# One decoder layer on one core: cache copies, token squares, key turns and value products rearranged

## What is computed

```python
z = rms_norm(x, g_pre) @ w_in
u = z[:, :512] * sigmoid(z[:, 512:1024])          # conv group
q, keys and values of three branches, gates = the rest of z
cy = silu(layer_norm(causal_depthwise_conv(u, 31 taps)))
# attention: compressed blocks, selected blocks, window of 512, gated sum
o  = g0 * attend(q, compress(k_cmp), compress(v_cmp)) \
   + g1 * attend(q, selected blocks) + g2 * attend(q, window)
h  = x + rms_norm(concat(cy, o) @ w_out, g_post)
y  = h + rms_norm(square(relu(rms_norm(h, g_pre2) @ w_up)) @ w_down, g_post2)
```

## Time and profile before

| what | value |
|---|---|
| device time, median of 3 runs | 873.06 us (871.01 to 876.92) |
| the profiled execution's own time | 874.44 us |
| span of the profiled execution, first to last instruction | 872.3 us |
| mean granted clock of PE | 0.959 of 2.4 GHz |
| busy: PE, PEld, DVE, ACT, POOL | 795.3, 726.9, 461.5, 241.6, 324.9 us |
| DMA, mean over the span | 98 GB/s, 85.47 MB |

### The profile page before, as it was taken

One profiled execution on the slowest core, in us unless ns is written; L12 is line 12 of the kernel. 1 busy time (PEld: TensorE's weight loads), 2 busy tenths in 40 slices (PEclk: granted clock), 3 DMA queues, 4 the chain that ended last, 5 costly groups with the idle time before them and its releaser, 6 DMA issues.

```text
span 872.3 us, 15023 instructions
## 1 busy us (share of the span) xinstructions
PE 795.3 (91%) x6285; PEld 726.9 (83%) x6285; DVE 461.5 (53%) x661; ACT 241.6 (28%) x432; POOL 324.9 (37%) x119
## 2 busy tenths in 40 slices
PE   4979999998996898999896999999999999999990
PEld 3979999876675875665895999999999999999990
DVE  3839998466535465788267943472003433332217
ACT  3412422222244246777212322130000221200020
POOL 2100000111120010000172377777776777777754
PEclk9899999789997899999998999999999999999995
DMA  8443240244450089300021122222222122222102
GB/s 320 186 205 101 107 146 14 78 151 134 149 179 36 1 312 61 90 1 1 2 98 48 55 92 96 96 98 96 96 96 85 60 97 96 96 97 96 48 1 98
DMA packets 24015, 85.47 MB, mean 98 GB/s; under 512 B 7216, under 2 KB 10848, under 8 KB 16736
## 3 DMA queue, kind: packets, MB, share of 16 engines
q1 hardware_dynamic: 16736, 62.13, 22.4%
q0 software_dynamic: 3456, 16.78, 5.4%
q10 hardware_dynamic: 3776, 5.89, 1.9%
HBM read 80.51 MB, written 8.47 MB: 102 GB/s over the span
## 4 chain that ended last, share of the span: by engine, by line
PE 74%; DVE 12%; issue 5%; ACT 5%; DMA 4%; SPq 0%; DVEq 0%; ACTq 0%
PE PB L1320 26%; PE PA L1320 25%; PE PB L1595 4%; DMA wraw<-wblk_dram 3%; PE PS L1647 2%; PE PR L1448 2%; PE PR L1692 2%; DVE smx L1183 1%; PE PS L1712 1%; PE PB L1704 1%; DVE rb L812 1%; PE PS L1464 1%; DVE yC L864 1%; DMA xT<-x_fm_dram 1%; PE PA L1433 1%
## 5 line engine op out<-in xcount | busy, mean ns | idle before, releaser
L397 POOL TENSOR_TENSOR wH<-wraw,zero 128x2048 fp32r<-128x2048 f32 x33 | 118.9, 3602 | 232.2 <-PE PB L1320 205.0
L400 POOL TENSOR_TENSOR wL<-wraw,wH 128x2048 fp32r<-128x2048 f32 x33 | 159.9, 4846 | 2.6
L864 DVE SCALAR_TENSOR_TENSOR yC<-uP,vec,yC 128x512 f32<-128x512 f32 (+1 forms) x135 | 83.8, 685 | 0.1
L1253 DVE TENSOR_TENSOR hL<-h,hH 128x520 f32 (+1 forms) x32 | 52.5, 1643 | 49.2 <-ACT hH L771 49.2
L1320 PE MATMUL PA<-hL,wH 128*128 128x260 f32 x256 | 72.2, 282 | 0.0
L1320 PE MATMUL PB<-hL,wH 128*128 128x260 f32 x256 | 72.2, 282 | 0.0
L1320 PE MATMUL PA<-hH,wL 128*128 128x260 f32 x256 | 72.2, 282 | 0.0
L1320 PE MATMUL PA<-hH,wH 128*128 128x260 f32 x256 | 72.2, 282 | 0.0
L1320 PE MATMUL PB<-hH,wL 128*128 128x260 f32 x256 | 72.2, 282 | 0.0
L1320 PE MATMUL PB<-hH,wH 128*128 128x260 f32 x256 | 72.2, 282 | 0.0
L436 POOL DMA_INDIRECT rks<-pool_ks_dram,idx x8 | 8.7, 1082 | 162.6 <-PE PA L1413 117.1
(11 more groups left out here) (384 smaller groups left out, 2168.0 us busy)
## 6 DMA issues: line engine op xcount, KB each, us to landing
wraw<-wblk_dram SPq DMA_DIRECT2D x47, 1024.0 KB, 4.8
xT<-x_fm_dram SPq DMA_DIRECT2D x4, 520.0 KB, 6.1
xT<-x_fm_dram SPq DMA_DIRECT2D x1, 2080.0 KB, 10.2
y_fm_dram<-xT SPq DMA_DIRECT2D x8, 260.0 KB
rkw<-cwk_dram SPq DMA_DIRECT2D x8, 256.0 KB, 2.7
s_win_dram<-cwk_dram ACTq DMA_DIRECT2D x1, 2044.0 KB
s_win_dram<-cwv_dram ACTq DMA_DIRECT2D x1, 2044.0 KB
p_rows_dram<-ktok ACTq DMA_DIRECT2D x4, 256.0 KB, 2.4
```

The costliest lines, as they stand in the source:

```text
L397: pool.tensor_tensor(wH[s][:, :], wraw[s][:, :], zero[:, :].broadcast_to([P, BW]), ALU.add)\
L400: pool.tensor_tensor(wL[s][:, :], wraw[s][:, :], wH[s][:, :].bitcast(F32), ALU.subtract)\
L864: dve.scalar_tensor_tensor(out=dst, in0=src, scalar=w, in1=first, op0=ALU.mult, op1=ALU.add)\
L1253: dve.tensor_tensor(lo, h2[c % 2][:, :], hi.bitcast(F32), ALU.subtract).then_inc(s_hl, 1)
```

## The change

Six edits in one step. **Squares:** all four x loads are issued before the first weight block; ACT squares all eight tiles; DVE adds them in pairs; PE sums four pairs; the first block is split behind the root and the reciprocal. **Cache copies:** ACT issues one before each half of the MLP. **Key turns:** the first two turns of a sequence are issued together, into banks 0 and 1, the third two steps later into bank 0; the key scores of the second sequence move into the next unit. **Conv tail:** ACT copies the selected scores out of `PA` at the end of the key units, and the mean, the subtraction, the squares, the root, the reciprocal and the scaling move into units 4 to 7. **Value products:** chunk n of a sequence goes to partitions 32 x (n mod 4) onward with 32 columns of `PT` instead of 8; two more buffers come from the raw rows' space (`rawc`); the new token's products and the sum over the four strips become matmuls at the second attention pair. **Blocks 13 and 14** are split inside the attention. The diff, cut:

```diff
@@ tiles
+        vsel = [rks[0], rks[1]] + [t_[:, 0:1024] for t_ in (KTb0, KTb1, *rawc)]
+        vwin = [rkw[0], rkw[1]] + [t_[:, 1024:1536] for t_ in (KTb0, KTb1, *rawc)]
+        VBUF = (0, 1, 2, 3, 4, 5, 0, 1)
@@ SP
-            load_x(0)
-            load_x(1)
+            for i in range(4):
+                load_x(i)
             sp.dma_start(wraw[0][:, :], A_wblk[B_IN]).then_inc(s_raw[0], 16)
-            load_x(2)
-            load_x(3)
...
+            for b in range(4, 6):
+                sp.wait_ge(s_xt, 4 * (b + 3))
+                value_window(b)
+            for b in range(6, NS):
+                sp.wait_ge(s_dpv, b - 5)
+                value_window(b)
             sp.wait_ge(s_cmm, 8)
             load(1, 13)
             load(0, 14)
@@ ACT
-            for k in (0, 1, 2, 3, 4, 6):
+            for k in range(KT):
                 act.wait_ge(s_x[k // 2], 16)
-                if k == 4:
-                    block_hi(B_IN)
                 act.activation(psq[k][:, :], xT[:, k, :], ACT.Square).then_inc(s_sq0, 1)
             root(0, PB)
+            block_hi(B_IN)
...
-            for kv in range(2):
-                act.dma_start(A["s_win"][kv][:, 0:WIN - 1, :], A["win_rows"][kv][:, 1:WIN, :]).then_inc(s_out, 16)
...
                     x_evac(u + 1, 2 * e)
+                    if e == 1:
+                        gelu(u)
                     key_evac(2 * u + e, 2)
                     x_evac(u + 1, 2 * e + 1)
-                gelu(u)
...
             act.activation(Sw[:, 0:WIN], PB[0:64, 0, :], ACT.Copy).then_inc(s_dA, 1)
+            act.activation(Ss[:, 0:PAST].rearrange("p (a n) -> p a n", a=2), PA[0:64, :, :], ACT.Copy).then_inc(s_dA, 1)
...
-            for b in (13, 14):
-                block_hi(b)
...
-            act.activation(od[:, :].rearrange("p (a b) -> p a b", a=2), PS[0:8, :, :], ACT.Copy).then_inc(s_dA, 1)
+            act.activation(od[:, :].rearrange("p (a b) -> p a b", a=2), PS[:, :, :], ACT.Copy).then_inc(s_dA, 1)
...
+                if s in (8, 16):
+                    block_hi(13 if s == 8 else 14)
...
             for fh in range(2):
+                act.dma_start(A["s_win"][fh][:, 0:WIN - 1, :], A["win_rows"][fh][:, 1:WIN, :]).then_inc(s_out, 16)
@@ DVE
-            for k in (5, 7):
-                dve.wait_ge(s_x[k // 2], 16)
-                dve.tensor_tensor(psq[k][:, :], xT[:, k, :], xT[:, k, :], ALU.mult).then_inc(s_sq0d, 1)
-            block_lo(B_IN)
+            for k in range(0, KT, 2):
+                dve.wait_ge(s_sq0, k + 2)
+                dve.tensor_tensor(psq[k][:, :], psq[k][:, :], psq[k + 1][:, :], ALU.add).then_inc(s_sqp, 1)
             dve.wait_ge(s_vec, 16)
             rinv(0)
+            block_lo(B_IN)
...
-                dve.tensor_copy(KTb[b % 2][:, 512:1024], PS[:, 0, :]).then_inc(s_ktD, 1)
+                dve.tensor_copy(KTb[b % 2][:, 512:1024], PS[:, 1, :]).then_inc(s_ktD, 1)
...
+                if s in (10, 18):
+                    block_lo(13 if s == 10 else 14)
@@ PE, squares
-            for k in range(KT):
...
+            for k in range(0, KT, 2):
+                pe.wait_ge(s_sqp, k // 2 + 1)
@@ PE, turn_keys
                 elif q == 1:
+                    if b >= 1:
+                        pe.wait_ge(s_ktD, b)
+                    else:
+                        pe.wait_ge(s_dV, DV_CMAX - 1)
+                    if b % 2 == 1 and b >= 3:
+                        pe.wait_ge(s_w2e, b // 2)
+                else:
                     pe.wait_ge(s_ktA, 2 * b + 1)
-                else:
-                    pe.wait_ge(s_ktD, b + 1)
...
-                    mm = pe.transpose(PS[:, 0, r * P:(r + 1) * P], src, ident[:, :])
+                    mm = pe.transpose(PS[:, q % 2, r * P:(r + 1) * P], src, ident[:, :])
@@ PE, between
+                if u <= 4 and jp == 1 and u >= 1:
+                    key_scores(2 * u - 1)
+                if u < 4 and jp == 5:
+                    key_scores(2 * u)
+                if u < 4 and jp % 4 == 1:
+                    turn_keys(2 * u + jp // 4, 0)
+                    turn_keys(2 * u + jp // 4, 1)
+                if u >= 1 and jp == (3 if u < 4 else 1):
                     cmp_out(u - 1)
...
+                if u < 4 and jp % 4 == 3:
+                    turn_keys(2 * u + jp // 4, 2)
...
-                if (u, jp) == (6, 4):
+                if (u, jp) == (4, 6):
                     mean_conv()
-                if (u, jp) == (7, 2):
+                if (u, jp) == (5, 2):
                     square_means(0)
                     square_means(1)
+                if (u, jp) == (5, 6):
+                    square_means(2)
+                    square_means(3)
@@ PE, value products
+                chunks = [(r * 64, vsel[VBUF[b]][:, r * P:(r + 1) * P]) for r in range(8)]
+                chunks += [(512 + r * 64, vwin[VBUF[b]][:, r * P:(r + 1) * P]) for r in range(4)]
+                chunks += [(768, vcS[:, b // 2, :])]
+                for n, (c0, rows) in enumerate(chunks):
+                    q = 32 * (n % 4)
+                    mm = pe.matmul(PS[q:q + 32, b // 4, (b % 4) * P:(b % 4 + 1) * P],
+                                   PT[:, c0 + b * 8:c0 + b * 8 + 32], rows, start=(n < 4), stop=(n >= len(chunks) - 4),
+                                   skip_group_check=True)
                 mm.then_inc(s_dpv, 1)
-                if b == 5:
+                if b == 6:
                     pe.wait_ge(s_cV, PC_DONE)
@@ PE, second pair
+                    for bi in range(2):
+                        pe.matmul(PR[:, 0, 0:64], vtok[0:8, bi, QT, :], PTn[0:8, bi * 64:(bi + 1) * 64],
+                                  start=(bi == 0), stop=False, skip_group_check=True)
                     for b in range(NS):
-                        mm = pe.transpose(PR[:, 0, b * 8:(b + 1) * 8], od[:, b * P:(b + 1) * P], ident[0:8, 0:8])
+                        mm = pe.matmul(PR[:, 0, b * 8:(b + 1) * 8], od[:, b * P:(b + 1) * P], osel[:, :],
+                                       start=False, stop=True, skip_group_check=True)
```

More of the change, by code:

```diff
@@ L351, in _ @@
             load(0, 14)
-            for b in range(4, NS):
-                sp.wait_ge(s_dpv, b - 3)
-                value_window(b)
-            sp.wait_ge(s_xt, 32)
+            sp.wait_ge(s_dpv, 6)
             sp.dma_start(xT[:, :, :], A["x_fm"]).then_inc(s_x2, 16)
@@ L669, in _, with square_conv @@
             gelu(4)
-            for i in range(4):
-                x_evac(6, i)
+            def square_conv(t):
+                act.wait_ge(s_tv, TV_XC + t)
+                if t >= 2:
+                    act.wait_ge(s_tp, t)
+                act.activation(sq[t % 2][:, :], yC[:, t, :], ACT.Square).then_inc(s_ta, 1)
+            square_conv(0)
+            square_conv(1)
+            x_evac(6, 0)
+            x_evac(6, 1)
+            square_conv(2)
+            square_conv(3)
+            x_evac(6, 2)
+            x_evac(6, 3)
+            gelu(5)
+            act.wait_ge(s_tp, 1 + CT)
+            act.activation(rb[:, :].rearrange("p (a b) -> p a b", a=2), PA[:, :, 0:HT], ACT.Sqrt, bias=epsc[:, :])\
+                .then_inc(s_ta, 1)
+            x_evac(7, 0)
+            x_evac(7, 1)
             act.wait_ge(s_dV, DV_SMAX)
@@ L680, in _ @@
             act.activation(Pc, Pc, ACT.Exp).then_inc(s_cX, 1)
[L681 to L692 removed]
+            x_evac(7, 2)
+            x_evac(7, 3)
             gelu(6)
[L694 to L695 removed]
             act.wait_ge(s_dP, DP_PTS)
@@ L1075, in tvi @@
                     dve.wait_ge(s_tv, tv[0])
+            for u in range(4):
+                key_evac(2 * u)
+                x_lo(u + 1, 0)
+                conv_some(3)
+                if u >= 1:
+                    cmp_out_evac(u - 1)
+                x_lo(u + 1, 1)
+                if u == 0:
+                    cv(dve.tensor_reduce(cmx, p3, AX.X, ALU.max))
+                    cv(dve.tensor_tensor(p3, p3, cmx.unsqueeze(2).broadcast_to([P, 32, 32]), ALU.subtract))
+                conv_some(3)
+                key_evac(2 * u + 1)
+                x_lo(u + 1, 2)
+                conv_some(4)
+                x_lo(u + 1, 3)
+                if u < 3:
+                    conv_some(4)
+            conv_some(TAPS * CT)
+            dve.memset(PT[:, 832:864], 0.0).then_inc(s_sel, 1)
+            dve.tensor_reduce(osel[:, :], ident[:, :].rearrange("p (j n) -> p n j", j=4)[:, 0:8, :], AX.X, ALU.add)\
+                .then_inc(s_sel, 1)
             cmp_out_evac(3)
             x_lo(5, 0)
+            sample_conv()
             x_lo(5, 1)
@@ L1083, in _ @@
             assert nv[0] == DV_CMAX
+            dve.wait_ge(s_tap, steps[0])
+            dve.wait_ge(s_ys, CT + 2)
+            tvi(dve.tensor_tensor(ysm[:, :], yC[:, 0, :], yC[:, 1, :], ALU.add))
+            tvi(dve.tensor_tensor(ysm[:, :], ysm[:, :], yC[:, 2, :], ALU.add))
+            tvi(dve.tensor_tensor(ysm[:, :], ysm[:, :], yC[:, 3, :], ALU.add))
+            assert tv[0] == TV_SUM
             x_lo(5, 2)
@@ L1093, in _ @@
```

(15 more changed lines are left out.)

132 lines of the change are left out of this document (33 added, 99 removed).

## The result

| kernel | median of the runs, us | ratio to before, 95% interval | profiled execution: time, span, mean clock |
|---|---|---|---|
| before | 873.13 of 5 (871.01 to 876.92) | 1 | 874.44, 872.3, 0.959 |
| changed | 850.13 of 5 (844.73 to 850.74) | 0.9726 [0.9702, 0.9751] | 844.73, 842.8, 0.960 |

The change saves 23.0 us by the medians, where 28.2 were forecast: inside the range, faster by over 1%. The profiled execution is the fastest of the five, and by it the change saves 29.7. That difference of some 6 us is granted clock: in each of the five runs the span times the mean clock is 809 to 810 us. The forecast's terms are compared with the profile first, stage by stage.

The account below looks back on a forecast made before the run. TensorE, busy nearly all the time, was taken as the bound, with gains only before 420 us. Terms -2.2 -7.0 -6.4 -6.5 -12.5 +1.4 +5.0 = -28.2 took 874.44 to 846.2, 844.8 us at the median's level; range 832 to 861.

Parts of the forecast that it names:

- Squares: Start of the kernel: first normalised tile at 18.0 instead of 20.2 us, -2.2; bounds -1 to -4.
- Cache copies: Input projection: without the late weight load the PE gap goes, -4.8, and half clock gives back 2.2; -7.0 us.
- Rival (3): MLP: a cache copy holds up a weight load as long as two did, +19 us, so 864; chance 0.09.
- Key turns: First four compression units: PE no longer waits for VectorE's copy of a turned key, -6.4 us; bounds -4 to -7.
- Units 4 to 7: Units with the conv tail moved in: waits 7.8 instead of 12.2 us, plus clock; together -6.5, bounds 0 to -10.7.
- I let it go with the waits, by 2.1: Units 4 to 7: of 5.5 us lost to half clock, 2.1 us go along with the removed waits.
- Value products: Value stage: 1.3 us a sequence on four strips, od's copy ends 17.9 us after stage start instead of 30.4; -12.5.
- Rival (1): Value products: four strips bring no more than two, 0.064 us a record, value term -10, time 847.2; chance 0.22.
- Rival (2): Value products: changing strips drains PE, 7.1 us a sequence, +28.1 instead of -12.5, time 885; chance 0.04.
- Strip sum, blocks 13 and 14: Attention: strip sum and new tokens +1.4 us; splits of both blocks between attention steps +5.0, bounds 0 and +8.4.
- The prediction's own sign of being wrong: Attention: a stage longer than 95 us, one of four listed signs that the forecast is wrong.
- Rival (4): Conv tail gives back what it took: units 4 to 7 gain nothing, splits cost 8.4 us, time 854.7; chance 0.15.

Follow-up runs that it names:

- Run tail: Changed kernel with only the order of units 4 to 7 rewritten so that PE's four waits there have no cause left; 838.99 us, ratio 0.9607.
- run two: Changed kernel with compressed keys copied out ahead of unit 0's first low halves, and value products on two strips instead of four; 845.76 us, ratio 0.9714.
- run strips: Changed kernel with value products of b=0 on one strip, b=2 on two neighbouring, b=3 on two apart, the others on four; one run, 852.44 us.
- run pieces: Changed kernel with blocks 13 and 14 split inside the attention in quarters of 512 columns, one a pair; 842.33 us, ratio 0.9666.
- run all: Changed kernel with units 4 to 7 reordered, own buffers for b=6 and b=7 rows, quartered splits, earlier compressed-key copy, probabilities turned behind b=1; 817.99 us.

## Why the prediction was right, and where it was wrong

*Squares.* The first normalised tile came at 18.8 where 18.0 was forecast: the sums take 5.60 us from the first pair on, since the pairs come one by one. The stage gained 3.0 in the profile, within the bounds; that the time gained it is not shown.

*Cache copies.* -7.0 forecast, -7.4 in the profile. Undoing it costs 9.3, PE gap and fall included. Rival (3) is dead: of the MLP's weight loads the slowest landed in 11.9 us, where the forecast allowed 15.7, and PE waited for none.

*Key turns.* -6.4 was too small. Without the chance fall and the moved scores the units 0 to 3 gain 13.5 - 2.9 - 2.7 = 7.9, and undoing costs 8.7 to 10.9. A unit takes 16.35 us where 16.8 was forecast; PE's idle time in these units fell by 6.2 us (6.4 to 0.2), and the rest is busy time.

*Units 4 to 7.* The step that failed is "I let it go with the waits, by 2.1". The waits came out nearly as walked (6.8 for 7.8), but half-clock time rose from 13.6 to 17.1 us in this profile, beside four waits of 1.0 to 2.5 us. With the 2.7 us of scores moved in, the stage gained 0.6 instead of 6.5; without them, 3.3. Run tail shows the mechanism: without the waits, no falls.

*Value products.* -12.5 forecast, -14.2 measured, and its working names the right chain: od ended 8.2 us behind the turn of the probabilities (285.1 to 293.3), the forecast's 7.2 and 0.9 that the copy waits for b=7. The pace was mis-sized (0.99 for 1.3 us). Rival (1), two strips, was priced 2.5 us above the forecast; in run two `od` is 3.1 us later behind the first product and the time +1.7 with an interval of 4.5. So the device time could not have told the likeliest case from this rival; run strips does, by its records. The landing of the last rows was taken as 5.4 and was 10.3; ACT's work covered all of it but one microsecond. Rival (2) is dead at 0.034 to 0.038 us a record. The Trainium skill (TensorE: Matmul & The Clock Gate, Wait — 56ns, not 53.3ns?) speaks of 62 ns a matmul in one decode mode; these records are faster, so that price does not apply here. The forecast read the attention's stream of before as no faster than that either, from 1.02 us for 16 records. Two lines of the same stream, with 8 and with 16 records, show 0.43 us for eight more, 0.054 a record:

```profile
347.28 0.66 PE L1712 MATMUL PS<-PTb,vtok 128*64 128x128 f32 x8
...
361.83 1.09 PE L1712 MATMUL PS<-PTb,vtok 128*64 128x128 f32 x16
```

That is near the 0.059 of two strips in run strips. The 2.38x for three strips of the Trainium skill (TensorE: Matmul & The Clock Gate, Part 3: Packing small matmuls), carried to four as an estimate of 0.9 us, agrees with 0.88 to 0.99.

*Strip sum, blocks 13 and 14.* +6.4 forecast, +12.9 measured. PE's idle time in the attention rose by 3.4 (12.4 for 9.0), so the insertions were priced too high as waits. The rest is busy time, +9.5, and most of it is the clock: 17.4 us of this window at half rate, 10.2 of them from 297.1 on, in the first pairs, and 3.4 behind each low half; in quarters (run pieces) these two are gone. The first is not explained: run all, where PE idles 1.3 us in the value stage instead of 5.2, still has 10.2 us of it. The strip sum took 2.49 (0.61 and 1.88) instead of 0.66, +1.8, nearer to its upper bound. The prediction's own sign of being wrong, an attention stage longer than 95 us, came true with 97.7. Here the forecast had no term for the clock at all; the window of before had shown 1.00, and I took that as given for work that puts new waits into it.

Rival (4), the conv tail that gives back what it took, came near in both of its places: units 4 to 7 gained 0.6, and the attention grew by 12.9. That the profile's sum, -29.4, still met the forecast is luck: keys and value products gained somewhat more than forecast, and 6.5 us come from the fall in the prompt's compression, which the profile of the kernel before has and the changed kernel's escaped. The median, 850.1, lies 5.3 us above the forecast; units 4 to 7 (+3.2 without the moved scores) and the attention (+6.5) are more than that, keys, value products and squares give part of it back. The low end of the range, 832, does not follow from the bounds named beside it: they add up to -37.4, which is 835.6. The result lies inside either way.

## What to carry to other kernels

Where PE runs at its full clock, price a new wait with what follows it: here waits of 1.4 to 2.5 us were followed in many executions, not in all, by stretches of 3.4 to 13.7 us at half clock. Between two profiles, taking the waits out of units 4 to 7 saved 13.7 us where 6.8 were idle, and 10.4 in the time. When a stage is made faster, walk the other engines to its end before sizing the gain: the late rows did not decide this one, but ACT's list of copies behind one turn, and the products' pace only through the moment at which that turn came. Work that has to stand on a critical engine is put there in pieces that fit the slack of a step.

## What the runs showed of the hardware that was not expected

- The same wait of 1.7 us at the prompt's compression was followed by 10.2 to 13.7 us at half clock in five profiles, and by none in five others. One profile is not enough to tell whether a kernel has such a fall; the spread of its runs (6.0 us in the changed kernel, 1.7 to 3.2 in the four with a wait of 0.5) hints at it.
- VectorE's scaling of a tile in SBUF took 4.46 us instead of 0.60 while POOL subtracted two SBUF tiles, and its maximum over PSUM was not held up (0.42 with and without). The Trainium skill (SBUF — State Buffer, Who interferes with whom) says that such an operation of VectorE and one of POOL can shut each other out for a whole instruction, and that a reduction does not take part; this trace agrees, with these numbers.
- Four strips of 32 columns, fp32, run at 0.034 us a record, against 0.114 on one; two neighbouring strips are as fast as two apart (0.059).
